# Column groups in the sample's merge, and layer 1's first norm and queries beside it, in a decoder trunk on one core

## What is computed

```
def run_trunk(x, c, ...):
    for layer in range(2):
        sh1, sc1, ga1, sh2, sc2, ga2 = split_mod(c, w_mod[layer], b_mod[layer], 6)
        h = modulate(rmsnorm(x, g_norm[layer, 0]), sh1, sc1)
        if layer == 0: y = s5_mixer(h, ...)
        else:
            q_lat, q_pe = mla_query(h, ...)
            y = mla_out(attend(q_lat, q_pe, ckv, kr), w_ukv, w_o)
        x = x + ga1 * y
        h = modulate(rmsnorm(x, g_norm[layer, 1]), sh2, sc2)
        x = x + ga2 * peer(h, peer_w_q[layer], peer_keys[layer], peer_u[layer], peer_v[layer])

def sample_attention(q_lat, q_pe, ckv_new, kr_new, cache_ckv, cache_kr, page_table):
    # per sample token: running maximum m, sum l and latent output acc over the pages, then the new row
    ...
    return acc / l

def mla_out(o_lat, w_ukv, w_o):
    o = einsum("blhc,chd->blhd", o_lat, w_ukv[..., QK_NOPE:])     # 16 heads of 64
    return o.reshape(.., 1024) @ w_o

def peer(h, w_q, sub_keys, u_emb, v_emb):
    q = (h @ w_q).reshape(tokens, 8, 2, 128)
    s = einsum("thsd,hsnd->thsn", q, sub_keys)
    # 16 best of each half, 16 best sums of the 256 pairs: 16 experts for each of 8 heads
    g = softmax(best_s)
    act = gelu(einsum("td,thkd->thk", h, u_emb[idx]))
    return einsum("thk,thkd->td", g * act, v_emb[idx])
```

## Time and profile before

| | us |
|---|---|
| median of 3 runs | 3672.77 (3669.32 to 3676.19) |
| the profiled execution | 3665.84 |
| its span | 3664.0 |
| PE busy | 2650.3 (72%) |
| DVE busy | 2367.8 (65%) |
| ACT busy | 1223.5 (33%) |
| POOL busy | 1307.2 (36%) |
| layer 1's gathers, first issue | 2304.19 |

### The profile page before, as it was taken

The page is one execution under the profiler, slowest core; times in us unless marked ns, Lnnn a source line. Parts: engine busy times, 40 slices in busy tenths (PEclk is TensorE's granted clock), DMA queues, the critical chain, the costliest instruction groups (busy, mean ns, idle before and its releaser), DMA issues.

```text
span 3664.0 us, 63101 instructions
## 1 busy us (share of the span) xinstructions
PE 2650.3 (72%) x24936; PEld 987.7 (27%) x24936; DVE 2367.8 (65%) x5633; ACT 1223.5 (33%) x3811; POOL 1307.2 (36%) x1153
## 2 busy tenths in 40 slices
PE   4564899867766866658789996777686668666676
PEld 3353632403200400012225664322031004001100
DVE  8645387687776677555553541878867766765645
ACT  1212133434333333334432220343343343333333
POOL 5300033444444444433413510334444444443432
PEclk7666899867766966769999997777787679777667
DMA  8755599999999999999962044899999999999997
GB/s 330 209 140 200 220 396 411 405 419 410 409 420 419 409 420 420 403 420 381 393 218 107 19 187 157 322 400 403 421 402 417 421 419 409 421 420 400 417 420 319
DMA packets 214367, 1276.43 MB, mean 348 GB/s; under 512 B 54568, under 2 KB 60080, under 8 KB 67208
## 3 DMA queue, kind: packets, MB, share of 16 engines
q0 software_dynamic: 151552, 1109.46, 74.2%
q1 hardware_dynamic: 61968, 162.67, 12.8%
q10 hardware_dynamic: 576, 0.59, 0.1%
HBM read 1258.85 MB, written 11.43 MB: 347 GB/s over the span
## 4 chain that ended last, share of the span: by engine, by line
DMA 35%; PE 35%; DVE 19%; ACT 5%; issue 4%; SPq 1%; DVEq 1%; POOL 0%; PEldq 0%; ACTq 0%; POOLq 0%
DMA arena<-peer_uv,arena 34%; PE psum L2522 12%; DVE arena L1981 8%; PE psum L2469 6%; PE psum L2430 3%; DVE arena L1598 3%; PE psum L2870 2%; PE psum L2601 1%; PE psum L2670 1%; DVE arena L1607 1%; ACT arena L1339 1%; ACT arena L1336 1%; DVE arena L1892 1%; DVE arena L1992 1%; ACT arena L1326 1%
## 5 line engine op out<-in xcount | busy, mean ns | idle before, releaser
L2522 PE MATMUL psum<-arena 32*32 32x512 f32 x16384 | 1528.0, 819 | 740.3 <-ACT arena L1339 733.7
L1101 POOL DMA_INDIRECT arena<-peer_uv,arena x1040 | 1136.4, 1093 | 2007.5 <-PE psum L2522 1536.6
L1981 DVE SCALAR_TENSOR_TENSOR arena<-arena 128x1024 f32<-128x1024 f32 x1040 | 1273.6, 1226 | 743.5 <-DMA arena<-peer_uv,arena 731.7
L2522 PEld LDWEIGHTS psum<-arena 32*32 32x32 f32 x16384 | 216.5, 119 | 1915.0 <-ACT arena L1339 1813.8
L1326 ACT ACTIVATE arena<-arena 128x1 f32<-128x1 f32 x1040 | 210.3, 202 | 1533.3 <-DVE arena L1981 1532.2
L1339 ACT ACTIVATE arena<-arena 128x32 f32<-128x32 f32 x1024 | 329.0, 321 | 33.4
L1336 ACT ACTIVATE arena<-arena 128x1 f32<-128x1 f32 x1040 | 306.0, 294 | 33.8
L2469 PEld LDWEIGHTS psum<-arena 128*128 128x128 f32 x2048 | 245.7, 198 | 72.5 <-issue 69.5
L2469 PE MATMUL psum<-arena 128*128 128x128 f32 x2048 | 263.4, 286 | 2.2 <-ACT arena L1279 2.2
L2327 PE MATMUL psum<-arena 128*9 128x128 f32 x2048 | 98.8, 374 | 111.3 <-DMA arena<-b_mod 111.3
L1598 DVE TENSOR_TENSOR arena<-arena 128x512 f32<-128x512 f32 (+8 forms) x182 | 149.7, 823 | 18.7 <-ACT arena L1169 5.6
(11 more groups left out here) (293 smaller groups left out, 2379.5 us busy)
## 6 DMA issues: line engine op xcount, KB each, us to landing
arena<-w_mod SPq DMA_DIRECT2D x64, 1024.0 KB
arena<-peer_wq SPq DMA_DIRECT2D x12, 2048.0 KB, 12.6
arena<-peer_uv,arena POOLq DMA_INDIRECT x1040, 10.4
arena<-w_glu SPq DMA_DIRECT2D x5, 2048.0 KB, 12.8
arena<-mod_rows SPq DMA_DIRECT2D x4, 1024.0 KB
arena<-w_o SPq DMA_DIRECT2D x1, 4096.0 KB
arena<-x_after_layer SPq DMA_DIRECT2D x7, 512.0 KB
arena<-w_uq SPq DMA_DIRECT2D x1, 3072.0 KB, 15.0
```

The lines of the kernel that those rows point to most:

```text
L1101: pool.indirect_dma_start(ring[r], None, a[f"peer_uv{t // 5}"], bass.IndirectOffsetOnAxis(ap=ix, axis=0)).then_inc(landed[r], 16)
L1981: dve.scalar_tensor_tensor(out=u, in0=u, scalar=1.0, in1=h, op0=ALU.mult, op1=ALU.mult, accum_out=at(DOTS + (t % 2) * 2 * P + m, 1)).then_ ...
L2522: ins = pe.matmul(acc_of(t, i, c), diag[rows, r, :], ring[r][rows, D + 512 * c:D + 512 * (c + 1)], start=(m == 0), stop=last, skip_group_c ...
```

## The change

Four edits.

1. Latent queries: the product's operands change sides. Head `4 * g + m` goes to the output partitions from 32 g on; ACT copies the result whole into SBUF, PE turns it back with eight transposes between the key and the value products, and ACT writes eight small copies into place; the second value product waits for these.
2. Tile 5's first norm leaves `peer_dve(1)` and goes into the loop over the cache blocks: SP loads the rows, scale, gain and shift of tile 5 apart (`FX`, `FSC`, `FSH`), ACT squares them in block 1 and takes the root in block 3, DVE works in blocks 1, 2, 4 and 5, and PE turns them in block 7. The steps are taken out of `PLAN[1]` by `EARLY`, up to the choice of head 0.
3. Tile 5's first query part and its score stand between PE's steps of the merge, ACT's copies of them likewise, and the six parts of head 0's choice stand on DVE ahead of `attention_out(4)`.
4. Latent outputs, heads and projection of the sample go into four column groups (heads 4 g to 4 g + 3, or 256 columns, to the partitions from 32 g on). `attention_out(4)` works on 128 x 256 instead of 8 x 1024; loads, gates and the store of the sample's rows come in four pieces. `sample_project` replaces `project(4)`.

Beside these the last two parts of the query weights are issued right after the sample's projection, ahead of its store; the keys get a semaphore of their own; layer 1's gains for the other tiles are applied in tile 6's norm.

The diff, cut to its core:

```diff
-        PLAN = [peer_plan(layer) for layer in range(2)]
+        EARLY = ([(what, 5) for what in ("squares", "means", "roots", "norm", "shifted", "turned")]
+                 + [("turn", 5, 0), ("turn", 5, 1), ("queried", 5, 0), ("score", 5, 0), ("scored", 5, 0)]
+                 + [("query", 5, 0, q) for q in range(4)] + [("top", 5, 0, part) for part in range(6)])
+        PLAN = [peer_plan(0), [step for step in peer_plan(1) if step not in EARLY]]
...
                     load(t0)
                     load(t0 + 1)
-                    peer_weights(1, 2)
-                    peer_weights(1, 3)
                     final_loads()
...
+                sp.wait_ge(s_rst[1], row_no(STORES, "residual", 3))
+                sp.dma_start(at(FX, D), x3_dram[0:P]).then_inc(s_fl, 16)
+                sp.dma_start(at(FSC, D), mod_dram[0:1, 10 * D:11 * D].partition_broadcast(P)).then_inc(s_fl, 16)
+                sp.dma_start(at(FSH, D), a["g_norm"][3:4, :].partition_broadcast(P)).then_inc(s_fl, 16)
+                sp.wait_ge(s_fm, 1)
+                sp.dma_start(at(FSH, D), mod_dram[0:1, 9 * D:10 * D].partition_broadcast(P)).then_inc(s_fl, 16)
 
                 sp.wait_ge(s_cs, NB)
                 peer_weights(1, 0)
                 peer_weights(1, 1)
                 sp.wait_ge(s_cpv, NB)
                 peer_keys(1)
                 sp.wait_ge(s_yy, 5)
+                peer_weights(1, 2)
+                peer_weights(1, 3)
                 attention_store(4)
...
                 for h in range(0, NH, 2):
                     act.wait_ge(s_ktp, h // 2 + 1)
                     act.activation(kt_[0:NOPE, h, :], psum[0:NOPE, h // 2 % 4, :], ACT.Copy).then_inc(s_kta, 1)
+                act.wait_ge(s_ql, 2)
+                act.wait_ge(s_qz, 1)
+                for m in range(4):
+                    for c in range(2):
...
+                    if b == 1:
+                        peer_squares(5)
+                    if b == 3:
+                        peer_roots(5)
                     act.wait_ge(s_cpv, b + 1)
                     act.activation(acc[:, b, :], psum[:, 7, 0:KVL], ACT.Copy).then_inc(s_col, 1)
+                peer_turned(5)
                 act.wait_ge(s_mg, 2)
                 act.activation(at(EX, 5 * 32, 0, NB), at(EX, 5 * 32, 0, NB), ACT.Exp).then_inc(s_mg, 1)
...
+                peer_queried(5, 0)
+                peer_scored(5, 0)
...
             def peer_norm(t):
...
+                if t == 6:
+                    dve.wait_ge(s_pmod, 80 + 48)
+                    link(peer_mods(1, P, HSP))
+                    link(peer_mods(1, NB, HSP))
...
+                    if b == 1:
+                        dve.wait_ge(s_fl, 48)
+                        dve.scalar_tensor_tensor(out=at(FSC, D), in0=at(FSC, D), scalar=1.0, in1=at(FSH, D),
+                                                 op0=ALU.add, op1=ALU.mult).then_inc(s_fm, 1)
+                        dve.wait_ge(s_fm, 1)
+                    if b == 2:
+                        peer_means(5)
+                    if b == 4:
+                        peer_norm(5)
+                    if b == 5:
+                        peer_shifted(5)
                 merge()
-                dve.wait_ge(s_os, 1)
-                dve.tensor_copy(at(OO, D, 0, NB), psum[0:NB, 0:2, :].rearrange("p b n -> p (b n)")).then_inc(s_on, 1)
+                dve.wait_ge(s_mg, 11)
+                dve.tensor_copy(at(OO, 256), psum[:, 0, 0:256]).then_inc(s_mg, 1)
+                link(dve.tensor_copy(at(HT + D, D), at(FX, D)))
+                for part in range(6):
+                    peer_top(5, 0, part)
                 attention_out(4)
...
-                for c in range(2):
-                    for h in range(NH):
-                        ins = pe.matmul(psum[:, 5, (c * NH + h) * NB:(c * NH + h + 1) * NB],
-                                        wkt[:, h, P * c:P * (c + 1)], qts[0:NOPE, h, :], start=True, stop=True)
+                for m in range(4):
+                    for g in range(4):
+                        h = 4 * g + m
+                        ins = pe.matmul(psum[32 * g:32 * g + NB, 4 + m // 2, KVL * (m % 2):KVL * (m % 2 + 1)],
+                                        qts[0:NOPE, h, :], wkt[:, h, :], start=True, stop=True, skip_group_check=True)
...
                     if b + 1 < NB:
                         for n_ in range(5, 9):
                             cache_turn(b + 1, n_)
+                    else:
+                        peer_turn(5, 0)
+                        peer_turn(5, 1)
                     pe.wait_ge(s_cTc, b + 1)
...
-                for c in range(2):
-                    for b in range(NB):
-                        out = psum[:, 4, (c * NB + b) * NH:(c * NB + b + 1) * NH]
-                        pe.matmul(out, acc[:, b, P * c:P * (c + 1)], at(SW + b * NH, NH), start=True, stop=False)
-                        ins = pe.matmul(out, at(KVR[0] + P * c, P, 0, NB), at(WNM + b * NH, NH, 0, NB),
-                                        start=False, stop=True)
+                for r in range(2):
+                    for g in range(4):
+                        b = 4 * r + g
+                        pe.matmul(psum[32 * g:32 * g + 32, 2, KVL * r:KVL * (r + 1)], at(SW + b * 32, 32), acc[:, b, :],
+                                  start=True, stop=False, skip_group_check=True)
...
+                ot = at(OTS, KD * NB).rearrange("p (k t) -> p k t", k=KD)
+                for k in range(KD):
+                    for g in range(4):
+                        ins = pe.matmul(psum[32 * g:32 * g + NB, 2, 0:256], ot[:, k, :],
+                                        wo[:, k, 256 * g:256 * (g + 1)], start=(k == 0), stop=(k == KD - 1),
+                                        skip_group_check=True)
                 ins.then_inc(s_yy, 1)
```

More of the change, by code:

```diff
@@ L242, in row_no @@
                     if row_slot(q, m) == slot and not (passes is LOADS and (q, m) in NOT_LOADED)]
-            return 16 * len(mine)
+            return 16 * sum(4 if row == ("residual", 4) else 1 for row in mine)
         ROUNDS = ([("u", r) for r in range(NR)] + [("k", r) for r in range(NR)]
@@ L1258, in peer_squares @@
                 R = rows_of(t)
+                if t == 5:
+                    act.wait_ge(s_fl, 48)
+                    act.activation(at(OTT, D), at(FX, D), ACT.Square, accum_out=stat[:, 1:2]).then_inc(s_sq, 1)
+                    return
                 if t < 2:
@@ L2703, in attention_pe @@
                 pe.wait_ge(s_qlc, 1)
+                for j in range(8):
+                    ins = pe.transpose(psum[:, 6 + j // 4, P * (j % 4):P * (j % 4 + 1)], at(MHT + P * j, P), ident)
+                ins.then_inc(s_ql, 1)
                 for i in range(NTILE):
+                    if i == 1:
+                        pe.wait_ge(s_qlc, 5)
                     if i >= 2:
@@ L2780, in attention_pe @@
                 pe.wait_ge(s_cnm, NB)
-                pe.transpose(psum[0:NB, 4, 0:P], at(NM, NB), ident)
-                pe.transpose(psum[0:NB, 4, P:2 * P], at(LSUM, NB), ident).then_inc(s_mg, 1)
+                pe.transpose(psum[0:NB, 0, 0:P], at(NM, NB), ident)
+                pe.transpose(psum[0:NB, 0, P:2 * P], at(LSUM, NB), ident).then_inc(s_mg, 1)
+                for q in range(2):
+                    peer_query(5, 0, q)
                 pe.wait_ge(s_mg, 4)
-                pe.transpose(psum[:, 5, 0:NB], at(EX, P, 0, NB), ident[0:NB, 0:NB]).then_inc(s_mg, 1)
+                pe.transpose(psum[:, 1, 0:NB], at(EX, P, 0, NB), ident[0:NB, 0:NB]).then_inc(s_mg, 1)
@@ L2793, in attention_pe @@
                 ins.then_inc(s_mg, 1)
+                peer_score(5, 0)
                 pe.wait_ge(s_mg, 8)
-                for h in range(NH):
-                    for c in range(2):
-                        ins = pe.matmul(psum[0:NB, h // 8, VH * (h % 8):VH * (h % 8 + 1)], olt[:, c, h, :],
-                                        wv[:, c, VH * h:VH * (h + 1)], start=(c == 0), stop=(c == 1))
-                ins.then_inc(s_os, 1)
-                project(4)
+                for j in range(4):
+                    ins = pe.transpose(psum[:, 3, P * j:P * (j + 1)], at(OO + P * j, P), ident)
@@ new lines, in attention_pe @@
+                ins.then_inc(s_mg, 1)
+                pe.wait_ge(s_mg, 10)
+                for m in range(4):
+                    for c in range(2):
+                        for g in range(4):
+                            h = 4 * g + m
+                            ins = pe.matmul(psum[32 * g:32 * g + NB, 0, VH * m:VH * (m + 1)], olt[:, c, h, :],
+                                            wv[:, c, VH * h:VH * (h + 1)], start=(c == 0), stop=(c == 1),
+                                            skip_group_check=True)
```

140 lines of the change are left out of this document (89 added, 51 removed).

## The result

The kernel after takes 3615.6 us (median of 3606.8, 3611.4 and 3619.9; one disturbed run of 6993.7 is left out), that of before 3671.1 in the runs beside it: a ratio of 0.9844, 95% interval 0.9819 to 0.9870, or 55 us less. The forecast was 3621 in 3600 to 3643. The profiled execution took 3606.81 us, its span is 3605.0. Busy are PE 2611.4 (before 2650.3), DVE 2367.2, ACT 1226.1, POOL 1303.8 us: PE lost 39 us of work, the others changed by under 4, and bytes rose from 1276.43 to 1278.53 MB.

What follows compares the result with a forecast made beforehand. Gather bytes bound layer 1's experts from 2304 us on; ahead of them a chain of waits through PE, DVE and ACT. Terms -10.5 - 42.5 + 1 = -52 off the median 3672.77 gave 3621, range 3600 to 3643.

Steps and rivals of the forecast that it cites:

- Part 1: Latent queries ahead of the keys: 16 products of 256 columns in column groups, -10.5 us, all reaching the end.
- if it holds: Key products behind the latent queries: PE's clock may stay up, 2.6 us more gain, sum -11.2; otherwise -8.6.
- Part 2: First norm inside the cache loop: all its steps fit into waits of DVE and ACT, 0 us.
- Rival (c): First norm holds up the cache loop, for example by a late load: +9 us, 3630; chance 0.06.
- Part 3: Merge with queries inside: first gather at 2245.0, 59 us earlier; last two query weights issued at 2240.9.
- Part 4: Start of the transfer-bound stretch: engines start 63.3 us earlier, less loads of 23.8 us, 3 absorbed by idle time: -42.5.
- +1 for the gains: Later tiles' modulation gains, now in tile 6's norm on DVE: 0 to +2.6 us, taken as +1.
- (a): PE's clock stays low through the chain to the first gather: -40 us, 3633; chance 0.12.
- (b): Late query weights starve the gather ring, transfer engines idle some 10 us: -42, 3631; chance 0.08.
- (d): Loads in the first expert tile cost nothing, as DVE's choice of heads paces it: -70 us, 3603; chance 0.07.
- (e): Expert stretch runs at a lower transfer rate, 392 GB/s, growing by 61 us: 3682, slower; chance 0.04.
- (f): Queries' wait holds the merge longer than column groups save; would need 50 us more; chance 0.01.

Runs made afterwards that it cites:

- groups only: Kernel after with tile 5's first norm, queries and head 0's choice back behind the sample's projection, all loads behind its store: 3635.6 us, ratio 0.9909.
- more bytes: Kernel after with the final gains (1.57 MB) loaded four times instead of once in layer 1's experts: ratio 0.9870.
- after again: Kernel after, unchanged, run again beside three other kernels on the same chip: ratio 0.9863 against before.

## Why the prediction was right, point by point

**Part 1** (-10.5): loops 275.8 to between 265.5 and 266.4 where undisturbed, -9.4 to -10.3. Right, and 0.2 to 1.1 too much. The key products took 15.70 in after, with the grant fallen, and 14.0 in six others: "if it holds" and "if it falls" both happen, from one execution to the next, and bear 1.7 on PE, not 2.6. At the end of the loops only 0.5 to 0.9 of the 1.7 are left, so "all of it reaches the end" is not quite true; where the rest goes was not looked for.

**Part 2** (0): held in seven of the eleven traces with the norm in the loop. Three of these have key products of 14.0 us and loops of 265.5 to 265.6, and groups only, with the same key products and no norm in the loop, has 265.8. In the other four the loops were 3 to 4 us longer, by a cause that is open. Rival (c) had its price at 9 and from a late load; that was never seen.

**Part 3** (first gather 38.7 after the first weights' issue, late weights 34.6): 39.5 and 34.5. The sum was right by terms that were not, and that they offset each other is luck. Too low: the second weight lands 12.9 us after its issue and not 11.6; two groups 6.63 for 6.0; latent outputs 2.2 for 1.86. Too high: heads 1.08 for 1.8, row copy 0.68 for 1.2, projection 3.64 for 5.3. The heads were bounded by the shortest row of another width (0.92 for 32 of 128 columns), and 64 columns a product cost less. By the Trainium skill, TensorEngine Tiling (Array Packing), section Tiling Modes, Key Properties, a change of tiling mode drains the TensorE. In after 32 records in four lots of changing form took 2.31 us, 32 of one form 1.94 in the same trace. That is 0.12 for each of three more changes, if the lots cost nothing else; the trace does not bear out a drain that would matter here.

**Part 4** (-42.5, and +1 for the gains): merge and experts together are 1412.4 us after, 1457.7 before, -45.3 for -41.5. The mechanism was right and is shown two ways (the bytes above, groups only), with more bytes pointing the same way. The term that was mis-sized is the room in the first tile: I took 3.2 us idle in one window of 20 us, and the first 46 us had 6.1. The +1 for the gains was not measured apart. With part 1 too large by 1 and part 4 too small by 4, the three stretches add to -54.8 for -52.

The late weights landed 13.1 us after issue, not 19, and two steps of that estimate failed. I let them share with the gathers from 5 us on, when the first gather was issued; but its first bytes moved 4.1 us later, and until 2236 the weights (queue 1) had the engines alone. And I let them share by halves of the bytes. Where both move, the trace has nearly as many packets of either queue, of 16 KB for the weights and 8 KB for the gathers on queue 0 (queue, packets, MB, share of the engines; 2232.13 to 2236, then 2237 to 2239):

```profile
q1 hardware_dynamic: 113, 1.59, 96.1%
```

```profile
q1 hardware_dynamic: 39, 0.64, 74.5%
q0 software_dynamic: 33, 0.27, 31.9%
```

In after again, 2248 to 2250, it is 35 packets to 37, 0.57 MB to 0.30. Round robin by the packet is what the Trainium skill states in DMA: Bandwidth & Descriptors, section Queues, rings and completion order. The trace agrees with it in the even counts, if what it counts is the page's packet, which no run here shows; the bytes go two to one with the size of the packet.

**Rivals.** (a) The clock was at 0.50 over the first two query groups, 2206 to 2212, and full from there to the first gather, as taken. (b) Not in after, where the ring's first place came free at 2251.18 and the transfers stayed at 1.01; true in the run that sends the weights out 14 us later, with 15 us of idle transfers for 10, and 26 us in all. That the place of two issues decides it stood nowhere in the prediction. (c) See part 2. (d) Fell with the 13 us given back. (e) Fell: 413 GB/s behind the first 46 us in both kernels. (f) Fell.

**What was not foreseen** is the wait itself as a thing to improve: 7.9 us of PE for a weight that the first two query groups never read. The prediction named it (5 us) and counted it as given.

## What to carry to other kernels

When work moves ahead of a stretch that is bound by transfers, count what stood in its shadow: here 72 us earlier at the first gather were 59 at the end, since 7.5 MB of loads that used to hide came along. The order of loads on a queue next to such a stretch can be worth more than the work that was moved: two lines made 26 us here, the early norm and queries 19 net. And where one wait covers several loads, ask which of them the next instruction reads.

## What the hardware showed that was not expected

Products of 16 columns bring PE's grant from 1.00 to 0.50 while PE is never idle (after 4.5 us at full clock), and under products of 8 columns it stays at 0.50 to their end. Products of 256 columns in column groups held it at the merge when they began at 1.00, and in groups only, where they began at 0.50, 4.1 us of them did not bring it back; at the latent queries it fell under or behind them in some traces and stayed in others. At the merge's wait for the weights, after 3.12 and 3.40 us of idle the grant had stayed and after 2.97 and 3.35 it had fallen; after 6.8 us and more it had fallen in all. An indirect gather's first bytes moved 4.1 us after its issue, and a plain load of 16 KB packets beside it got twice its bytes. And a start that is identical in code lies anywhere from 1926.4 to 1938.3, so that effects under 10 us are to be read from stretches of the trace.
